# Experts in seven items instead of eight, three of them of 64, 32 and 32 places, with condition rows and experts' pieces fetched earlier

## The chip, the cores and the metric

The kernel runs on one core of a Trainium2 chip. The metric is the device time of one execution in microseconds (us), lower is better. All arithmetic is 32-bit float.

## The reference

Two groups of 128 tokens (context and latent) of width 1024 go through two layers with shared weights. Each layer computes a modulation from a condition vector, mixes tokens in three branches (differential attention, a long convolution, retention), projects, and ends in a mixture of 16 experts, which is what the change is about:

```python
def moe(h, w_router, b_router, w1, w3, w2):
    ...
    gate = ...          # top-1 group of four, top-2 experts inside it, per token
    a = jnp.einsum('bld,edf->blef', h, w1)          # D_MODEL 1024, D_FF 512
    b = jnp.einsum('bld,edf->blef', h, w3)
    act = jax.nn.silu(a) * b * gate[..., None].astype(h.dtype)
    return jnp.einsum('blef,efd->bld', act, w2)
```

With 256 tokens and two experts per token, an expert gets 32 tokens on average, and every expert's 6 MB of weights are needed in each layer.

## The kernel before

**Pieces and slots.** All weights come in pieces of 128 x 2048 floats (1 MB), fetched by SP (`fetch`, L578 to L585) in one fixed order, `PLAN` (L116): modulation pieces (`ada`), the projections (`proj`, units 0 to 29), six merges, four output units, four pieces of modulation part 5, then the 96 pieces of the experts (`moe`). `ring_table` (L138) gives each piece a slot and the count of `s_weights_used` that TensorE must have reached before the slot may be overwritten. There are 8 ring slots (`SLOTS`) and 6 lent ones (`LENT`), the latter made of tiles of the token-mixing stage. Dense pieces use the first 5 ring slots (`LEAST`), the opening's pieces all 8; the experts' pieces use all 14, the lent ones once the last merge is done (`END["merge", layer, 5]`). SP issues in order: a wait for one piece holds all behind it. Before the experts SP also waits for the stores of the stage before (`s_stored`, L596) and for the last chunk (`s_chunk_used`, L597).

**Chunks.** Ring slots 5 to 7 hold, during the token mixing, the condition rows, broadcast to 128 partitions (`cond_wide`, `raw`, L439 to L441), and the landings of 64 chunks of modulation weights, which DVE multiplies with the rows (`make_parts`, L1753). SP fetches chunks between dense pieces (`fetch_chunk`, L566); the first waits for `s_cond_ready` 2. In the opening POOL fetches the rows (L655) once all pieces of the opening are used (`MADE_FREE`, L654), ACT takes their tanh after unit 1 of the convolution (L1452), and DVE finishes them after unit 2 and its decay tables (L1886 to L1890).

**Opening of TensorE.** `first_units_of_first` (L822) computes units 0 to 3 as the modulation comes in, then `proj` (L794) runs units 4 to 29 with banks 0 to 3 in turn; DVE frees a bank when it has applied the convolution's taps to the unit.

**Experts.** Tokens are routed, experts 0 to 11 are sorted by their number of tokens (`sort`, L2217), and the work is cut into eight items (L42 to L50). An item is 128 places, which TensorE uses as stationary columns:

- a pair: two experts with 64 places each (items 0 and 1 the unsorted experts 12 to 15; items 4 to 6 sorted places 1 to 6)
- wide: the largest expert with 128 places (item 2)
- quad: the four smallest with 32 places each (item 3)
- single: one expert with 64 places (item 7), its weights split in two halves that run side by side in 64 columns each (`moe_in_extra` L1108, `moe_out_extra` L1151)

For each item `gather` (L1062) brings the tokens to their places; `moe_in` (L1087) multiplies them with the four pieces of w1 and w3 per expert in four quarters (two halves times banks 6 and 7), eight k-steps each, in each step one matmul per expert:

```python
for k in range(KT):
    for j in range(many):
        rows = slice(width * j, width * j + width)
        last = pe.matmul(bank[b][rows, half * 256:half * 256 + 256],
                         hgat[:, k, rows], w[j][:, k, :], ...)
```

ACT (tanh, L1630) and DVE (L2341, L2345) form the activation, `act_turn` (L1123) transposes it, `moe_out` (L1130) multiplies with the two pieces of w2 per expert in two halves of four f-steps, 512 columns each, and `combine` (L1175) adds the item to the output banks 0 to 3 through a matrix of places and gates. TensorE's order is in item p, gather p + 1, turn p, out p - 1 and combine (L1284 to L1298); in layer 0 it also does steps of the next layer's filter in items 3 to 6. The chain `seats`, `picks` (L2180, L2203) makes the place matrices on DVE, one pair of small operations per group and expert. An expert with more tokens than its room (`rooms`, L2241: 128 for the largest, 32 for the four smallest, else 64) gets extra blocks of 64 (`more_block`), which none does with these inputs.

`w[j]` of item p can be overwritten only after the whole quarter, since TensorE reports `many` pieces at once (L1106, L1143).

Of the kernel before, what the change touches and what calls it, by code (L numbers as in the profile page):

```python
# [17 lines left out]
ALU = mybir.AluOpType  # L18
# [3 lines left out]
P = 128  # L22
# [19 lines left out]
ITEM_KINDS = ("pair", "pair", "wide", "quad", "pair", "pair", "pair", "single")  # L42
# [3 lines left out]
ITEM_EXPERTS = ((12, 13), (14, 15), (0,), (8, 9, 10, 11), (1, 2), (3, 4), (5, 6), (7,))  # L46
# [3 lines left out]
ITEM_LAST = [2 if kind == "single" else len(e) for kind, e in zip(ITEM_KINDS, ITEM_EXPERTS)]  # L50
WIDE_ROOM, SMALL_ROOM = 128, 32

MORE = 2 * TOK // (BLOCK + 1)
# [26 lines left out]
LANDINGS = 3  # L80

# [56 lines left out]
def ring_table():  # L138

    pieces = [(item, c) for item in PLAN for c in range(PLAN_PIECES[item[0]])]  # L140
    done = [(item, c) for item in DONE for c in range(PLAN_PIECES[item[0]])]
    gone = {piece: n + 1 for n, piece in enumerate(done)}
    free, filled = [0] * (SLOTS + LENT), [0] * (SLOTS + LENT)
    slot, count, used = [], [], []
    for (kind, layer, _), c in pieces:
        lent = range(SLOTS, SLOTS + LENT) if kind == "moe" else ()
        own = SLOTS if kind == "moe" or (kind, layer, _) in OPENING else LEAST
        since = {at: free[at] for at in range(own)}
        since.update({at: max(free[at], END["merge", layer, 5]) for at in lent})
# [5 lines left out]
        free[at] = gone[(kind, layer, _), c]  # L155
    return slot, count, used
# [4 lines left out]
MADE_FREE = max(END[item] for n, item in enumerate(OPENING))  # L161
# [34 lines left out]
def y_end(layer, p, half):  # L196

    if p == PAIRS:
        return END["moe", layer, 0]
    return ff_end(layer, p + 1) + ITEM_OUT[p] // 2 * (half + 1)  # L200
# [92 lines left out]
def trunk_program(nc, row_scratch, cond_scratch, weights, mod_weights, cond_rows, experts, mod_params, params, consts, shared, x_in, k_cache, v_cache, s_cache,  # L293
                  y_out, k_out, v_out, s_out):
    with ExitStack() as ctx:
# [264 lines left out]
        def _(sp):  # L560
# [3 lines left out]
            chunk = 0  # L564

# [12 lines left out]
            def fetch(source):  # L578
                nonlocal n
                if USED[n]:  # L580

                    sp.wait_ge(s_weights_used, USED[n])
                slot = ring[:, SLOT[n], :] if SLOT[n] < SLOTS else lent[:, SLOT[n] - SLOTS, :]
                sp.dma_start(slot, source).then_inc(s_weights_in[SLOT[n]], 16)
                n += 1  # L585

            for kind, layer, number in PLAN:
                if kind != "moe":
# [7 lines left out]
                sp.wait_ge(s_stored, 16 * 4 * (layer + 1))  # L596
                sp.wait_ge(s_chunk_used, sum(CHUNKS[:layer + 1]))  # L597
# [8 lines left out]
                for p in range(ITEMS):  # L606
# [7 lines left out]
                    for part in (0, 2, 1, 3) if ITEM_KINDS[p] == "single" else range(4):  # L614
                        for j in range(many):
                            fetch(expert(p, j, part))
# [4 lines left out]
                for part in (4, 5):  # L621
                    fetch(expert(PAIRS, 0, part))
# [7 lines left out]
        def _(pool):  # L630
# [15 lines left out]
            for layer in range(DEPTH):  # L646
# [49 lines left out]
        def _(pe):  # L696
# [390 lines left out]
            def moe_in(layer, p):  # L1087
# [5 lines left out]
                width = P // many  # L1093
                for half in range(2):
                    for b in (6, 7):
# [12 lines left out]
            def moe_in_extra(layer):  # L1108

                pe.wait_ge(s_hgat_lo, ITEMS * layer + PAIRS + 1)  # L1110
                pe.wait_ge(s_hgat_hi, ITEMS * layer + PAIRS + 1)
                for b in (6, 7):
                    take(b)
                    w = piece(256), piece(256)
                    for k in range(KT):
                        for j in range(2):
                            last = pe.matmul(bank[b][64 * j:64 * j + 64, 0:256],  # L1117
                                             hgat[:, k, 64 * j:64 * j + 64], w[j][:, k, :],
                                             start=(k == 0), stop=(k == KT - 1),
                                             skip_group_check=True)  # L1120
                    last.then_inc(s_weights_used, 2)

            def act_turn(layer, p):  # L1123
                pe.wait_ge(s_act_ready, ITEMS * layer + p + 1)
                take(6)
                for f in range(4 if p < PAIRS else 2):
# [3 lines left out]
            def moe_out(layer, p):  # L1130
# [3 lines left out]
                width = P // many  # L1134
                for half in range(2):
                    w = [piece(512) for _ in range(many)]
                    take(5 - half)
                    for f in range(4):
                        for j in range(many):
                            rows = slice(width * j, width * j + width)  # L1140
# [3 lines left out]
                if p == 0:  # L1144
                    for b in range(4):
                        take(b)
                last = combine(s_y_lo, ITEMS * layer + p + 1, s_y_hi, PAIRS * layer + p + 1,
                               s_scat_ready, scat[p % 3], p == 0)
                last.then_inc(s_combined, 1)

            def moe_out_extra(layer):  # L1151

                n = ITEMS * layer + PAIRS + 1
                pe.wait_ge(s_actT_ready, n)
                w = piece(512), piece(512)
                take(5)
                for f in range(4):
                    for j in range(2):
                        last = pe.matmul(bank[5][64 * j:64 * j + 64, :],
                                         actT[PAIRS % 2][:, f % 2, 64 * (f // 2):64 * (f // 2) + 64],  # L1160
                                         w[j][:, f, :], start=(f == 0), stop=(f == 3),
                                         skip_group_check=True)
                last.then_inc(s_weights_used, 2)
                pe.wait_ge(s_scat_ready, n)
                pe.wait_ge(s_y_lo, n)
                for j in range(2):
                    r = slice(64 * j, 64 * j + 64)
                    for t in range(4):
                        last = pe.matmul(bank[2 * j + t // 2][:, (t % 2) * TOK:(t % 2 + 1) * TOK],
                                         ysb[r, t * P:(t + 1) * P], scat[PAIRS % 3][r, :],  # L1170
                                         start=False, stop=False, skip_group_check=True)
                        if t % 2:
                            last.then_inc(s_combined, 1)

            def combine(lo, count, hi, hi_count, scat_event, matrix, fresh):  # L1175
                pe.wait_ge(scat_event, count)
                for dt in range(KT):
                    if dt == 0:
                        pe.wait_ge(lo, count)
                    if dt == 4:  # L1180
# [4 lines left out]
                                     skip_group_check=True)  # L1185
                return last
# [42 lines left out]
            for layer in range(DEPTH):  # L1229
# [91 lines left out]
        def _(act_e):  # L1321
# [82 lines left out]
            for layer in range(DEPTH):  # L1404
# [40 lines left out]
                for u in range(U_HY, U_HY + 6):  # L1445
# [6 lines left out]
                    if layer == 0 and u == 1:  # L1452
# [173 lines left out]
                for p in range(ITEMS):  # L1626
                    n = ITEMS * layer + p
                    sc_e.wait_ge(s_weights_used, ff_end(layer, p) - ITEM_LAST[p])
                    wide = 512 if p < PAIRS else 256
                    sc_e.activation(th[:, 0:wide], bank[6][:, 0:wide], ACT.Tanh, scale=0.5).then_inc(  # L1630
                        s_ff_tanh, 1)
# [3 lines left out]
                    sc_e.activation(flat(actT[p % 2])[:, 0:wide], bank[6][:, 0:wide],  # L1635
                                    ACT.Copy).then_inc(s_actT_ready, 1)
# [33 lines left out]
        def _(dve):  # L1670
# [140 lines left out]
            for layer in range(DEPTH):  # L1811
# [60 lines left out]
                for u in range(U_HY, U_HY + 6):  # L1872
# [307 lines left out]
                def seats(p):  # L2180

                    many = 2 if ITEM_KINDS[p] == "single" else len(ITEM_EXPERTS[p])
                    ranks_, gates_ = (rank, gate) if p < FIXED_ITEMS else (sorted_rank, sorted_gate)
                    for g in range(GROUPS):
                        for j in range(many):
                            e = ITEM_EXPERTS[p][j % len(ITEM_EXPERTS[p])]
                            width = P // many
                            yield (g, slice(width * j, width * j + width), C("xf")[:, 0:width],
# [52 lines left out]
                def rooms():  # L2241
# [5 lines left out]
                    link(ts(extra, at, SORTED - 4.5, ALU.is_gt, float(SMALL_ROOM - BLOCK), ALU.mult))  # L2247
# [9 lines left out]
                def out_high(p):  # L2257
# [5 lines left out]
                    dve.wait_ge(s_y_hi, PAIRS * layer + p + 1)  # L2263
# [62 lines left out]
                for p in range(ITEMS):  # L2326
                    n = ITEMS * layer + p
                    wide_ff = 512 if p < PAIRS else 256
# [10 lines left out]
                    if n:  # L2339
                        dve.wait_ge(s_act_turned, n)  # L2340
                    link(stt(act[:, 0:wide_ff], th[:, 0:wide_ff], 1.0, bank[6][:, 0:wide_ff], ALU.add,  # L2341
                             ALU.mult))
                    dve.sem_inc(s_bank_free[6], 1)
                    dve.wait_ge(s_weights_used, ff_end(layer, p))
                    tt(act[:, 0:wide_ff], act[:, 0:wide_ff], bank[7][:, 0:wide_ff],  # L2345
                       ALU.mult).then_inc(s_act_ready, 1)
# [14 lines left out]
                    if p == PAIRS - 1:  # L2361
                        dve.wait_ge(s_more_known, layer + 1)
                        blocks = dve.value_load(ints[0:1, 0:1], min_val=0, max_val=MORE)

# [169 lines left out]
```

## Time and profile before

| | before |
| --- | --- |
| median of 3 runs | 1211.95 us (1210.23 to 1212.96) |
| the profiled execution, its own time | 1209.46 us |
| its span in the profile | 1207.7 us |
| mean granted TensorE clock, share of full speed | 0.978 |
| TensorE matmul busy (x records) | 1144.6 us (x6966) |
| VectorE busy | 510.8 us (42%) |
| ScalarE busy | 215.3 us (18%) |
| bytes moved by DMA | 351.51 MB, mean 291 GB/s |
| SP's fetches of experts' pieces | 108 to ring, 84 to lent slots, 1024 KB each |
| condition rows, issue to landing | 6.2 us |

PE is TensorE's matmul, PEld its weight load, DVE VectorE, ACT ScalarE, POOL GpSimd, SP SyncE; a `q` behind a name is the engine's sequencer. L1102 is line 1102. The profile shows each f32 matmul as two records, and their ends are modelled, so starts are the safer reading. PEclk is the TensorE clock that was granted (1.00 is 2.4 GHz). The chain lists what held the end, in order of time; a DMA in it counts from issue to landing.

### The profile page before, as it was taken

The numbers are of one execution on the slowest core, as the hardware profiler recorded it, in microseconds if no ns is written. First come the engines' busy times: TensorE is split into PE (matmuls) and PEld (weight loads), VectorE is DVE, ScalarE is ACT, GpSimd is POOL, SyncE is SP. The second block draws the span as 40 slices with busy tenths as digits, with TensorE's granted clock in tenths as the row PEclk, the third lists the DMA queues.
The fourth block names the chain that finished last, engine by engine and source line by source line (L and its number), as shares of the span: only waits on it lengthen the run. The fifth ranks groups of instructions, "written<-read, shape, count | busy, mean of one in ns | idle before, by whom it ended". The sixth has DMA issues, their size and how long they took to land.

```text
span 1207.7 us, 17513 instructions
## 1 busy us (share of the span) xinstructions
PE 1144.6 (95%) x6966; PEld 883.0 (73%) x6966; DVE 510.8 (42%) x1154; ACT 215.3 (18%) x452; POOL 41.2 (3%) x83
## 2 busy tenths in 40 slices
PE   6978999999999999989989999999999999998996
PEld 5667888878888775646548888888888877564653
DVE  2539877666736221111233876653252531111113
ACT  2240012232021100111124201223201210000011
POOL 1001110000000000000000111000000000000000
PEclk9998999999998999989999999999999899998999
DMA  9519874365459999999964578543434999999992
GB/s 384 219 70 347 310 283 172 142 261 223 183 205 423 421 421 386 422 420 421 420 261 161 180 279 276 188 161 132 139 140 177 418 421 420 371 422 420 421 420 101
DMA packets 55799, 351.51 MB, mean 291 GB/s; under 512 B 6960, under 2 KB 7136, under 8 KB 18336
## 3 DMA queue, kind: packets, MB, share of 16 engines
q1 hardware_dynamic: 51552, 337.75, 70.7%
q0 software_dynamic: 4160, 12.58, 2.8%
q8 instruction: 58, 0.95, 0.3%
q14 instruction: 29, 0.24, 0.1%
HBM read 346.08 MB, written 2.65 MB: 289 GB/s over the span
## 4 chain that ended last, share of the span: by engine, by line
PE 83%; DMA 11%; DVE 3%; ACT 2%; issue 1%; SPq 1%; DVEq 0%; ACTq 0%; POOLq 0%
PE bank L806 24%; PE bank L1102 12%; PE bank L1141 7%; PE bank L986 7%; PE bank L1007 5%; PE bank L801 5%; PE bank L1082 4%; PE bank L1182 4%; DMA lent<-in_experts 4%; DMA ring<-in_experts 4%; DMA ring<-in_weights 3%; PE bank L817 2%; PE bank L730 1%; PE bank L1117 1%; PE bank L1058 1%
## 5 line engine op out<-in xcount | busy, mean ns | idle before, releaser
L806 PE MATMUL bank<-h,ring 128*128 128x256 f32 x1472 | 327.4, 382 | 13.1 <-DMA ring<-in_weights 13.1
L806 PEld LDWEIGHTS bank<-h,ring 128*128 128x128 f32 x1472 | 279.0, 191 | 54.2 <-DMA ring<-in_weights 13.5
L1770 DVE SCALAR_TENSOR_TENSOR ring<-ring 128x1024 f32<-128x1024 f32 x128 | 151.7, 1223 | 17.5 <-DMA ring<-in_mod_weights 8.9
L1102 PE MATMUL bank<-lent,gates 128*64 128x256 f32 (+2 forms) x896 | 127.0, 380 | 2.3 <-ACT gates L1610 2.3
L1102 PE MATMUL bank<-ring,gates 128*64 128x256 f32 (+2 forms) x1024 | 121.0, 380 | 6.2 <-DMA ring<-in_experts 4.8
L1102 PEld LDWEIGHTS bank<-lent,gates 128*64 128x64 f32 (+2 forms) x896 | 82.6, 137 | 36.3 <-ACT gates L1610 2.8
L1102 PEld LDWEIGHTS bank<-ring,gates 128*64 128x64 f32 (+2 forms) x1024 | 80.0, 130 | 30.6 <-issue 6.8
L1141 PE MATMUL bank<-ring,gates 128*64 128x512 f32 (+2 forms) x304 | 83.7, 613 | 9.5 <-DMA lent<-in_experts 9.5
L1690 DVE SCALAR_TENSOR_TENSOR gates<-gates,bank 128x512 f32<-128x512 f32 (+1 forms) x16 | 10.5, 654 | 141.3 <-issue 108.9
L2262 DVE COPY uc<-bank 128x512 f32<-128x512 f32 x14 | 9.7, 692 | 132.4 <-PE bank L1141 132.4
L1141 PEld LDWEIGHTS bank<-ring,gates 128*64 128x64 f32 (+2 forms) x304 | 24.5, 135 | 54.2 <-issue 54.2
L1082 PE MATMUL bank<-uc,gates 128*128 128x128 f32 x512 | 60.4, 276 | 0.1
L1082 PEld LDWEIGHTS bank<-uc,gates 128*128 128x128 f32 x512 | 58.6, 192 | 0.7 <-DVE uc L1686 0.4
L986 PE MATMUL bank<-lent,ring 128*128 128x256 f32 x256 | 56.4, 380 | 0.0
L801 PE MATMUL bank<-ring,h 128*128 128x256 f32 x256 | 56.2, 379 | 0.0
L1007 PE MATMUL bank<-uc,ring 128*128 128x256 f32 x256 | 55.6, 379 | 0.0
L1141 PE MATMUL bank<-lent,gates 128*64 128x512 f32 (+2 forms) x176 | 55.0, 688 | 0.0
L1007 PEld LDWEIGHTS bank<-uc,ring 128*128 128x128 f32 x256 | 48.6, 190 | 6.6
L986 PEld LDWEIGHTS bank<-lent,ring 128*128 128x128 f32 x256 | 48.5, 190 | 6.5
L1182 PEld LDWEIGHTS bank<-gates,uc 128*128 128x128 f32 x224 | 41.6, 190 | 15.9 <-issue 10.8
L817 PE MATMUL bank<-h,ring 128*128 128x256 f32 x192 | 46.6, 403 | 6.6 <-ACT h L1346 6.6
L801 PEld LDWEIGHTS bank<-ring,h 128*128 128x128 f32 x256 | 48.2, 190 | 6.3
(268 smaller groups left out, 1141.8 us busy)
## 6 DMA issues: line engine op xcount, KB each, us to landing
ring<-in_experts SPq DMA_DIRECT2D x108, 1024.0 KB, 21.2
ring<-in_weights SPq DMA_DIRECT2D x96, 1024.0 KB, 6.5
lent<-in_experts SPq DMA_DIRECT2D x84, 1024.0 KB, 19.9
ring<-in_mod_weights SPq DMA_DIRECT2D x64, 512.0 KB, 5.6
lent<-lent POOLq DMA_DIRECT2D x48, 32.0 KB, 5.6
cst<-in_consts POOLq DMA_DIRECT2D x1, 1345.0 KB, 11.6
x<-in_x_in SPq DMA_DIRECT2D x1, 1024.0 KB, 5.0
ring<-in_cond_rows POOLq DMA_DIRECT2D x1, 1024.0 KB, 6.2
```

The lines of the kernel that those rows point to most:

```text
L730: last = pe.matmul(bank[b][32 * j:32 * j + 32, 0:256], condT[:, k, :], w[j][:, k, :], start=(k == 0), stop=(k == KT - 1), skip_group_check ...
L801: last = pe.matmul(bank[b][:, g * 256:(g + 1) * 256], h[:, k, g_cols(g)], w[:, k, :], start=(k == 0), stop=(k == KT - 1))
L806: last = pe.matmul(bank[b][:, c * TOK:(c + 1) * TOK], w[:, k, c * P:(c + 1) * P], h[:, k, :], start=(k == 0), stop=(k == KT - 1))
L817: last = pe.matmul(bank[u][:, c * TOK:(c + 1) * TOK], w[:, k, c * P:(c + 1) * P], h[:, k, :], start=(k == 0 and c == 0), stop=(k == KT - 1 ...
L986: last = pe.matmul(bank[b][:, c * TOK:(c + 1) * TOK], w[:, k, d * P:(d + 1) * P], src[:, k, :], start=(k == 0), stop=(k == 3))
L1007: last = pe.matmul(out[c], w[:, k, c * P:(c + 1) * P], merged[:, k, :], start=(k == 0), stop=(k == KT - 1))
L1058: last = pe.matmul(bank[b][:, c * P:(c + 1) * P], h[:, k, g_cols(n // 2)], ident, start=True, stop=True)
L1082: last = pe.matmul(bank[4 + half][:, c * P:(c + 1) * P], htok[:, g, k * P:(k + 1) * P], pick[p % 2][:, g, :], start=(g == 0), stop=(g == 1))
L1102: last = pe.matmul(bank[b][rows, half * 256:half * 256 + 256], hgat[:, k, rows], w[j][:, k, :], start=(k == 0), stop=(k == KT - 1), skip_g ...
L1141: last = pe.matmul(bank[5 - half][rows, :], actT[p % 2][:, f, rows], w[j][:, f, :], start=(f == 0), stop=(f == 3), skip_group_check=True)
L1182: last = pe.matmul(bank[dt // 2][:, (dt % 2) * TOK:(dt % 2 + 1) * TOK], ysb[:, dt * P:(dt + 1) * P], matrix, start=(fresh and dt % 2 == 0) ...
L1770: last = dve.scalar_tensor_tensor(out, w, 0.5, cond_wide[:, c, :], ALU.mult, ALU.mult, accum_out=mod_all[:, of, row, c:c + 1])
```

## The change

- Eight items become seven: pair, pair, triple, wide, triple, pair, triple. A triple is one expert with 64 places and two with 32, in columns 0 to 63, 64 to 95 and 96 to 127. Quad and single are gone, with `moe_in_extra` and `moe_out_extra`. The number of pieces stays 96 per layer; an item's share is 4 per expert in and 2 out.
- The six smallest sorted experts have room 32 instead of the four smallest.
- The last item's combine reports each bank by itself.
- The opening's pieces use ring slots 0 to 4 and lent slots 0 to 2, so that slots 5 to 7 are free for the condition rows. POOL fetches these after `END["ada", 0, 1]`; the cache loads into the lent tiles wait for the opening's end. ACT's tanh comes after unit 0, DVE's step after unit 1, ahead of unit 2 and the decay tables.
- Modulation part 5 may use slots 5 to 13 like the experts, once the last merge is done. The wait for the stores moves ahead of it, the wait for the chunks ahead of the first piece that goes to slots 5 to 7.

```diff
-ITEM_KINDS = ("pair", "pair", "wide", "quad", "pair", "pair", "pair", "single")
+ITEM_KINDS = ("pair", "pair", "triple", "wide", "triple", "pair", "triple")
+WIDTHS = {"pair": (64, 64), "triple": (64, 32, 32), "wide": (128,)}
...
-ITEM_EXPERTS = ((12, 13), (14, 15), (0,), (8, 9, 10, 11), (1, 2), (3, 4), (5, 6), (7,))
+ITEM_EXPERTS = ((12, 13), (14, 15), (1, 6, 7), (0,), (2, 8, 9), (4, 5), (3, 10, 11))
...
+OPENING_LENT = (SLOTS, SLOTS + 1, SLOTS + 2)
...
-    for (kind, layer, _), c in pieces:
-        lent = range(SLOTS, SLOTS + LENT) if kind == "moe" else ()
-        own = SLOTS if kind == "moe" or (kind, layer, _) in OPENING else LEAST
-        since = {at: free[at] for at in range(own)}
-        since.update({at: max(free[at], END["merge", layer, 5]) for at in lent})
+    for (kind, layer, number), c in pieces:
+        since = {at: free[at] for at in range(LEAST)}
+        if (kind, layer, number) in OPENING:
+            since.update({at: free[at] for at in OPENING_LENT})
+        elif kind == "moe" or (kind, number) == ("ada", 5):
+            since.update({at: max(free[at], END["merge", layer, 5]) for at in range(LEAST, SLOTS + LENT)})
...
-MADE_FREE = max(END[item] for n, item in enumerate(OPENING))
+OPENING_END = max(END[item] for item in OPENING)
...
+        if SLOT[n] in range(LEAST, SLOTS) and not given[layer]:
+            sp.wait_ge(s_chunk_used, sum(CHUNKS[:layer + 1]))
+            given[layer] = True
...
+        if (kind, number) == ("ada", 5):
+            sp.wait_ge(s_stored, 16 * 4 * (layer + 1))
...
-        sp.wait_ge(s_stored, 16 * 4 * (layer + 1))
-        sp.wait_ge(s_chunk_used, sum(CHUNKS[:layer + 1]))
...
-        pool.wait_ge(s_weights_used, MADE_FREE)
         pool.dma_start(raw, cond_rows.broadcast_to([P, 2 * D])).then_inc(s_cond_moved, 16)
-        pool.wait_ge(s_mod_ready, ada_at(0, 1) + 1)
+        pool.wait_ge(s_weights_used, OPENING_END)
...
-        for j in range(many):
-            rows = slice(width * j, width * j + width)
+        for j, rows in enumerate(ITEM_ROWS[p]):
...
+        if by_bank and dt % 2 and dt < KT - 1:
+            last.then_inc(s_combined, 1)
...
-        for p in range(PAIRS):
+        for p in range(ITEMS):
             moe_in(layer, p)
-            gather(layer, p + 1)
+            if p < PAIRS:
+                gather(layer, p + 1)
...
-        moe_in_extra(layer)
-        act_turn(layer, PAIRS)
-        moe_out(layer, PAIRS - 1)
-        moe_out_extra(layer)
+        moe_out(layer, PAIRS)
...
-        if layer == 0 and u == 1:
+        if layer == 0 and u == 0:
...
-            if layer == 0:
-                dve.wait_ge(s_cond_tanh, 2)
-                stt(flat(cond_wide), flat(cond_wide), 1.0, raw, ALU.add, ALU.mult).then_inc(
-                    s_cond_ready, 1)
-                dve.wait_ge(s_cond_ready, 2)
+        if layer == 0 and u == 1:
+            dve.wait_ge(s_cond_tanh, 2)
+            stt(flat(cond_wide), flat(cond_wide), 1.0, raw, ALU.add, ALU.mult).then_inc(
+                s_cond_ready, 1)
+            dve.wait_ge(s_cond_ready, 2)
...
-        many = 2 if ITEM_KINDS[p] == "single" else len(ITEM_EXPERTS[p])
         ranks_, gates_ = (rank, gate) if p < FIXED_ITEMS else (sorted_rank, sorted_gate)
         for g in range(GROUPS):
-            for j in range(many):
-                e = ITEM_EXPERTS[p][j % len(ITEM_EXPERTS[p])]
-                width = P // many
-                yield (g, slice(width * j, width * j + width), C("xf")[:, 0:width],
+            for e, rows in zip(ITEM_EXPERTS[p], ITEM_ROWS[p]):
+                yield (g, rows, C("xf")[:, 0:rows.stop - rows.start],
...
-        link(ts(extra, at, SORTED - 4.5, ALU.is_gt, float(SMALL_ROOM - BLOCK), ALU.mult))
+        link(ts(extra, at, SORTED - SMALL - 0.5, ALU.is_gt, float(SMALL_ROOM - BLOCK), ALU.mult))
```

## Rows read from the trace of the kernel before

**Rows 1.** The page, busy time, share of the span and records of TensorE's matmuls

```profile
PE 1144.6 (95%) x6966; PEld 883.0 (73%) x6966; DVE 510.8 (42%) x1154; ACT 215.3 (18%) x452; POOL 41.2 (3%) x83
```

**Rows 2.** The chain that ended last, opening: start us, us, what

```profile
40.87 3.66 PE bank L730 x64
...
66.20 6.18 DMA ring<-in_cond_rows
...
90.40 5.54 DMA ring<-in_weights
```

**Rows 3.** Timeline, opening: start us, us, engine line op tiles, shapes [idle before, releaser]

```profile
74.21 1.00 ACT L1449 ACTIVATE uc<-bank,par 128x256 f32<-128x256 f32 x2
...
87.71 2.29 DVE L1690 SCALAR_TENSOR_TENSOR ring<-ring 128x2048 f32<-128x2048 f32 x1
...
95.99 16.42 PE L806 MATMUL bank<-h,ring 128*128 128x256 f32 x64 [13.09 <-DMA ring<-in_weights]
```

**Rows 4.** Windows: stretch, length, busy PE PEld DVE ACT POOL, PEclk, DMA share, GB/s

```profile
83.00:96.00 13.00, 0.01 (x1) 0.01 (x1) 8.88 (x13) 5.21 (x16) 0.51 (x1) 0.66 0.38 143
430.00:440.00 10.00, 10.00 (x49) 7.64 (x44) 3.61 (x17) 0.00 (x0) 0.00 (x0) 1.00 1.01 420
```

**Rows 5.** The chain that ended last, from the merges to the experts of both layers

```profile
329.12 6.99 PE bank L986 x32
...
386.50 14.03 PE bank L1102 x128
...
406.30 14.03 PE bank L1102 x128
...
424.71 7.02 PE bank L1141 x32
431.73 3.65 PE bank L1182 x16
435.38 13.81 PE bank L1102 x64
...
464.09 3.63 PE bank L1102 x64
...
617.04 2.94 PE bank L1169 x16
...
964.10 14.03 PE bank L1102 x128
...
1193.96 4.16 PE bank L790 x16
```

**Rows 6.** SP's timeline at the first expert's piece; landings of L584, 300 to 640

```profile
357.32 1.53 SPq L584 DMA_DIRECT2D ring<-in_experts  x3
...
DMA to landing us min/median/max: 4.7/18.3/29.3
```

**Rows 7.** Timeline of TensorE at four changes of line (PE matmul, PEld weight load)

```profile
448.60 0.59 PE L1102 MATMUL bank<-ring,gates 128*128 128x256 f32 x2
448.82 0.36 PEld L1072 LDWEIGHTS bank<-cst,uc 128*128 128x128 f32 x2
...
463.50 0.59 PE L1182 MATMUL bank<-gates,uc 128*128 128x256 f32 x2
464.02 0.42 PE L1102 MATMUL bank<-ring,gates 128*32 128x256 f32 x3
...
464.02 0.12 PEld L1102 LDWEIGHTS bank<-ring,gates 128*32 128x32 f32 x3 [0.33 <-issue]
...
431.13 0.60 PE L1141 MATMUL bank<-lent,gates 128*64 128x512 f32 x2
431.66 0.48 PE L1182 MATMUL bank<-gates,uc 128*128 128x256 f32 x1
...
327.63 1.24 PE L986 MATMUL bank<-lent,ring 128*128 128x256 f32 x5
328.71 0.27 PE L1017 MATMUL bank<-cst,sm 128*16 128x128 f32 x1
```

More of the change, by code:

```diff
@@ L49 @@
 ITEM_OUT = [2 * len(e) for e in ITEM_EXPERTS]
-ITEM_LAST = [2 if kind == "single" else len(e) for kind, e in zip(ITEM_KINDS, ITEM_EXPERTS)]
-WIDE_ROOM, SMALL_ROOM = 128, 32
-MORE = 2 * TOK // (BLOCK + 1)
+ITEM_ROWS = [[slice(sum(WIDTHS[kind][:j]), sum(WIDTHS[kind][:j + 1])) for j in range(len(WIDTHS[kind]))]
+             for kind in ITEM_KINDS]
+WIDE_ROOM, SMALL_ROOM, SMALL = 128, 32, 6
+MORE = 8
 OVER = (TOK - 1 - SMALL_ROOM) // BLOCK + 1
@@ L154, in ring_table @@
         used.append(since[at])
-        free[at] = gone[(kind, layer, _), c]
+        free[at] = gone[(kind, layer, number), c]
     return slot, count, used
@@ L198, in y_end @@
     if p == PAIRS:
-        return END["moe", layer, 0]
+        return END["moe", layer, 0] - ITEM_OUT[p] // 2 * (1 - half)
     return ff_end(layer, p + 1) + ITEM_OUT[p] // 2 * (half + 1)
@@ L564, in _ @@
             chunk = 0
+            given = [False] * DEPTH
             def fetch_chunk():
@@ L613, in _ @@
                                                         max_val=SORTED - 1)
-                    for part in (0, 2, 1, 3) if ITEM_KINDS[p] == "single" else range(4):
+                    for part in range(4):
                         for j in range(many):
@@ L621, in _ @@
                 for part in (4, 5):
-                    fetch(expert(PAIRS, 0, part))
+                    for j in range(len(ITEM_EXPERTS[PAIRS])):
+                        fetch(expert(PAIRS, j, part))
             for c in range(4):
@@ L1106, in moe_in @@
                         last.then_inc(s_weights_used, many)
[L1108 to L1121, printed above, removed]
             def act_turn(layer, p):
@@ L1125, in act_turn @@
                 take(6)
-                for f in range(4 if p < PAIRS else 2):
+                for f in range(4):
                     last = pe.transpose(bank[6][:, f * P:(f + 1) * P], act[:, f * P:(f + 1) * P], ident)
@@ L1133, in moe_out @@
                 many = len(ITEM_EXPERTS[p])
-                width = P // many
                 for half in range(2):
@@ L1138, in moe_out @@
                     for f in range(4):
-                        for j in range(many):
-                            rows = slice(width * j, width * j + width)
+                        for j, rows in enumerate(ITEM_ROWS[p]):
                             last = pe.matmul(bank[5 - half][rows, :], actT[p % 2][:, f, rows], w[j][:, f, :],
@@ L1146, in moe_out, with combine @@
                         take(b)
-                last = combine(s_y_lo, ITEMS * layer + p + 1, s_y_hi, PAIRS * layer + p + 1,
-                               s_scat_ready, scat[p % 3], p == 0)
+                last = combine(s_y_lo, ITEMS * layer + p + 1, s_y_hi, ITEMS * layer + p + 1,
+                               s_scat_ready, scat[p % 3], p == 0, p == PAIRS)
                 last.then_inc(s_combined, 1)
[L1151 to L1175, printed above, removed]
+            def combine(lo, count, hi, hi_count, scat_event, matrix, fresh, by_bank=False):
                 pe.wait_ge(scat_event, count)
@@ L1627, in _ @@
                     n = ITEMS * layer + p
[L1628 to L1631, printed above, removed]
+                    sc_e.wait_ge(s_weights_used, ff_end(layer, p) - len(ITEM_EXPERTS[p]))
+                    sc_e.activation(th, bank[6][:, :], ACT.Tanh, scale=0.5).then_inc(s_ff_tanh, 1)
                     if p + 1 < ITEMS:
@@ L1634, in _ @@
                     sc_e.wait_ge(s_act_turned, n + 1)
-                    sc_e.activation(flat(actT[p % 2])[:, 0:wide], bank[6][:, 0:wide],
-                                    ACT.Copy).then_inc(s_actT_ready, 1)
+                    sc_e.activation(flat(actT[p % 2]), bank[6][:, :], ACT.Copy).then_inc(s_actT_ready, 1)
                     sc_e.wait_ge(s_actT_ready, n + 1)
@@ L2262, in out_high @@
                     dve.tensor_copy(ysb[:, 512:1024], bank[4][:, :]).then_inc(s_y_hi, 1)
-                    dve.wait_ge(s_y_hi, PAIRS * layer + p + 1)
+                    dve.wait_ge(s_y_hi, ITEMS * layer + p + 1)
                     dve.sem_inc(s_bank_free[4], 1)
@@ L2327, in _ @@
                     n = ITEMS * layer + p
-                    wide_ff = 512 if p < PAIRS else 256
                     if p + 1 < ITEMS:
@@ L2340, in _ @@
                         dve.wait_ge(s_act_turned, n)
-                    link(stt(act[:, 0:wide_ff], th[:, 0:wide_ff], 1.0, bank[6][:, 0:wide_ff], ALU.add,
-                             ALU.mult))
+                    link(stt(act, th, 1.0, bank[6][:, :], ALU.add, ALU.mult))
                     dve.sem_inc(s_bank_free[6], 1)
                     dve.wait_ge(s_weights_used, ff_end(layer, p))
-                    tt(act[:, 0:wide_ff], act[:, 0:wide_ff], bank[7][:, 0:wide_ff],
-                       ALU.mult).then_inc(s_act_ready, 1)
+                    tt(act, act, bank[7][:, :], ALU.mult).then_inc(s_act_ready, 1)
                     dve.wait_ge(s_act_ready, n + 1)
@@ L2363, in _ @@
                         blocks = dve.value_load(ints[0:1, 0:1], min_val=0, max_val=MORE)
+                out_high(PAIRS)
                 def more_block(layer, i):
```

2 lines of the change are left out of this document (removed).

## Prediction

> **What bounds the kernel now.** I read the page's shares first, then the chain that ended last, the timeline of the opening, the windows, and last single matmuls. TensorE is busy 95% of the span [rows 1]: its stream is the path, except where something holds it, and the chain shows where. In the opening the chain leaves TensorE for the condition rows' DMA (66.20 for 6.18), comes through decay tables to one DVE step of 2.29 that ends at 90.00, and goes back by a weight piece issued at 90.40 and landed in 5.54 [rows 2, 3]. TensorE idles 13.09 us of it, and since its clock falls to 0.66 [rows 4] its next 64 matmul records take 16.42 us [rows 3] instead of the 13.81 that 64 of this shape take elsewhere [rows 5]. In the experts' stage (386.50 to 619.98, 233.5 us; in the second layer 964.10 to 1193.96, 229.9 us) the chain is TensorE again [rows 5], while transfers run at 420 GB/s with a DMA share of 1 [rows 4], so that a piece of 1.049 MB takes 2.50 us. This stage has two limits close together: its matmuls, and its 96 pieces.
>
> The profile counts each f32 matmul as two records. A pair (two experts of 64 places side by side) has 128 records in 14.03 us, the wide item 64 in 13.81, a quarter of the quad 64 in 3.63 [rows 5]. So two or four narrow matmuls of one width run at once, and an item costs one full array's time, whatever it holds. The change builds on that.
>
> **Part 1, the opening.** SP stands before its first chunk until the condition step is done; the next dense piece is queued behind it [rows 2]. Now the rows' DMA waits only for the second modulation part, done at 44.5 [rows 2], 21.7 us before 66.20. It lands at 44.5 + 6.2 = 50.7, or, with two dense pieces in flight, at 55.7. ACT's tanh now follows unit 0 and may delay unit 1 by about 1 us; DVE's 2.29 follow unit 1, still before unit 2's matmuls end (about 65.6). So the piece that held TensorE can go out near 64 and land 5.5 us later, before TensorE asks for it at 95.99 - 13.09 = 82.90. Late next is the rest of DVE's chain: from 74.21 [rows 3] to 90.00 less the 2.29 moved out, now begun at 65.6, so unit 3's bank is free after its 2.03 us of taps near 81.2, and TensorE wants it at 89.8. Gain 13.1 + (16.4 - 13.8) = 15.7. Bounds: 10.9, if TensorE runs into DVE, whose own shift is only 90.00 - 79.1, and 15.7, which I take. POOL's cache loads stay behind the opening as they were. The opening's pieces sit in three lent slots in place of ring slots, the same number: nothing.
>
> **Part 2, earlier pieces.** SP issues in order; today it passes the last modulation pieces one by one behind the output projection, and the first expert's piece leaves at 357.32 [rows 6]. Now ten pieces may go when the last merge is done, 336.11 [rows 5]; the waits for stores and chunks that move ahead with them are satisfied earlier. But there are 14 slots, all full by then: later pieces wait for item 0's first quarter, done at 390.0. Today's queue reaches the fifteenth expert piece at 357.3 + 14 x 2.5 + 1.8 (the parameters' 0.75 MB) = 394. So 4 us of the 21 are left, for transfers alone. On a path bound by TensorE they are worth 0; if transfers set the end they are already in rival 1. POOL's two broadcasts of 512 KB share the queue, and TensorE needs their work 30 us later: 0.
>
> **Part 3, seven items, if a triple cost as much as a pair.** Without waits for DMA: item 0 takes 19.8 (386.50 to 406.30), a later one with a pair in and a pair out 29.1 (406.30 to 435.38), with the wide item in 28.7 (435.38 to 464.09) [rows 5], out of the wide 28.9; the last in-step has no gather behind it, 14.0 + 1.2 (the turn, no longer hidden) + 7.0 + 3.65 = 25.9; the last out 7.0 + 0.8 (copy) + 3.65 = 11.5. In all 19.8 + 29.1 + 29.0 + 28.7 + 28.9 + 29.0 + 25.9 + 11.5 = 201.9, and with 4.4 for filter steps in layer 0 206.3. Against 229.9 and 233.5: -28.0 and -27.2. Combining bank by bank adds only increments; a triple's 12 picks instead of 8 lie on DVE, busy 3.61 of 10 us [rows 4]; layer 1's first dense pieces now wait for half of the last out, still 12 us before they are used: 0 each. The routing of the reference's inputs puts at most 28 (layer 0) and 23 tokens (layer 1) on the six smallest sorted experts, so rooms of 32 call no extra block.
>
> **Part 4, what a triple costs.** It alternates 64, 32 and 32 columns, which no row shows. But each change of shape can be read. Full to full: records start 0.21 apart, and the weights of the next load at 448.82, 0.01 after the last record's start at 448.81. Full to 32 columns: 463.71 to 464.02, 0.31, and its LDWEIGHTS starts no earlier than its matmul. 64 columns to full, 512 moved: 431.14 to 431.66, 0.52 where 0.43 is usual [rows 7]. The surcharge is the same 0.09 whether 32 or 128 columns are to be loaded, so it isn't the load; it looks like a stop until the old shape has left the array. One row speaks against it: a transpose of 16 columns follows full matmuls after 0.22, with no gap [rows 7].
>
> If 64 to 32 is such a change, the 64 never overlaps the 32s. A k-step is 0.216 + 0.31 + 0.216 + 0.31 = 1.05 us instead of 0.44; 32 of them take 33.6, not 14.03: +19.6. An out-step is 2 x 0.43 + 2 x 0.52 = 1.90; 8 of them 15.2, not 7.02: +8.2. Together 27.8 per triple, 83.4 per layer. From below the cost is 0 (full overlap). From above each change waits for a matmul's whole 0.38 us, 5.7 more per triple: 33.5. I take 27.8: of all rows, those of a change are nearest. The Trainium skill, "TensorEngine Tiling (Array Packing)", Tiling Modes, says that changing the tiling mode, not just the tile, drains the engine, and lists 128x64 and 128x32 as two modes: by this rule the sum stands as it is. The same section calls tiles independent, loading and multiplying in parallel; by that alone a triple costs a pair, and the sum is rival 1's.
>
> **Sum**, against this execution's 1209.46 (span 1207.7): layer 0 -27.2 + 83.4 = +56.2, layer 1 -28.0 + 83.4 = +55.4, opening -15.7: +95.9, 1305.4. The median shown lies 2.5 above that execution: 1308.
>
> **Rival 1, the widths overlap (faster).** For: pairs and quads do, and the three tiles share no column. Against: no weights are loaded ahead across a change of shape. Then transfers decide. At 390.0 there are 82 pieces to issue; the last lands at 390.0 + 4.7 (the shortest landing [rows 6]) + 81 x 2.50 = 597.2, and half an out 3.5, copy 0.8 and combine 3.65 follow: 605.2 for 619.98, -14.8. Layer 1: 967.6 + 4.7 + 202.5 + 8.0 = 1182.8 for 1193.96, -11.2. With the opening 1167.8, as a median 1170 (1150 if slots and transfers never bind; 1192 with added waits and a lower clock). Its opposite begins where a triple costs (27.2 + 28.0 + 15.7) / 6 = 11.8 us more than a pair: beyond that point the change is slower.
>
> **Rival 2, overlap with a surcharge.** 2 x 0.09 in each of 32 + 8 steps, 7 us per triple: the stage takes 206.3 + 21 = 227, so some 5 us less than now, or the same with its waits. The opening alone is sure: 1209.5 - 15.7, median 1196 (1175 to 1212).
>
> **Rival 3, one width after the other, no stop.** A k-step 0.87 and an out-step 1.74: +20.7 per triple, 34.9 + 34.1 - 15.7: median 1265. It is the low end of my own case.
>
> **Chances.** The forecast, with rival 3 inside it, 0.57; its own range is 1255 to 1342. Rival 1 0.32. Rival 2 0.09, 0.01 of it within 0.2%, which is what a measurement of this kernel can tell from nothing. Anything else 0.02, half of it same, half slower. So faster 0.40, same 0.02, slower 0.58. The range has to hold rival 1: 1160 to 1335, with under 0.1 outside it.
>
> **What would show it.** Right: in a triple, starts 0.22 and 0.31 apart in turn, a quarter of 8.4 us with 48 records, LDWEIGHTS of the first 32 beside its own matmul, the DMA share under 0.9 in triples, no TensorE wait near 83. Rival 1: quarters of 3.5 us, 420 GB/s to the stage's end, and TensorE waiting for pieces in the last item. The forecast is wrong if a triple's quarter takes under 6 us; part 1 if TensorE still waits for a dense piece before 110.

## The result and the profile after

The changed kernel takes 1321.03 us (median; 1319.96 to 1322.32), the kernel before 1211.09 us (1208.37 to 1212.96): a ratio of 1.091, 95% interval 1.088 to 1.094. It is slower. The forecast was 1308 (range 1160 to 1335), and slower with a chance of 0.58. The profiled execution took 1322.08 with a span of 1320.3, against 1305.4 in the prediction's sum.

The page's line of busy time, to be held against [rows 1]:

```profile
PE 1285.1 (97%) x6862; PEld 869.6 (66%) x6862; DVE 505.6 (38%) x1140; ACT 210.5 (16%) x442; POOL 41.0 (3%) x83
```

TensorE has 104 records fewer than before and is busy 140.5 us longer, so a record takes longer on average.

The chain that ended last, from the experts of layer 0 and the triples' place in layer 1 (start us, us, what), which answers to [rows 5]:

```profile
368.94 14.03 PE bank L1108 x128
...
407.15 7.02 PE bank L1130 x32
...
417.82 36.21 PE bank L1108 x192
...
469.08 13.81 PE bank L1108 x64
...
487.12 15.88 PE bank L1130 x48
...
1061.76 36.21 PE bank L1108 x192
...
1307.23 3.54 PE bank L798 x16
```

A pair still takes 14.03 into the hidden layer and 7.02 out of it, the wide item 13.81. A triple takes 36.21 and 15.88, together 52.09. From its first experts' matmul to what follows its last combination, layer 0's stage runs from 368.94 to 667.65 and layer 1's from 1012.88 to 1307.23: 298.7 and 294.4 us, 65.2 and 64.5 more than before.

Inside a triple, the timeline of TensorE's weight loads and, further on, of its matmuls out of the hidden layer (start us, us, engine line op tiles, shapes, count, idle before):

```profile
420.01 0.19 PEld L1108 LDWEIGHTS bank<-ring,gates 128*64 128x64 f32 x2 [0.41 <-issue]
420.59 0.14 PEld L1108 LDWEIGHTS bank<-ring,gates 128*32 128x32 f32 x4 [0.39 <-issue]
421.15 0.19 PEld L1108 LDWEIGHTS bank<-ring,gates 128*64 128x64 f32 x2 [0.41 <-issue]
...
487.05 1.62 PE L1130 MATMUL bank<-ring,gates 128*64 128x512 f32 x3
488.06 0.62 PE L1130 MATMUL bank<-lent,gates 128*32 128x512 f32 x1
...
489.04 1.62 PE L1130 MATMUL bank<-ring,gates 128*64 128x512 f32 x3
```

One k-step goes from 420.01 to 421.15 (1.131 by the records' exact starts), one f-step from 487.05 to 489.04. The two 32s load together (four weight loads in 0.14 us), but the 64 stands by itself: the widths take turns, and the loads of the new width start only when the turn comes.

Windows of after (stretch, length, busy PE PEld DVE ACT POOL, PEclk, DMA share, GB/s), as [rows 4]:

```profile
83.00:96.00 13.00, 13.00 (x62) 11.45 (x61) 12.13 (x22) 1.31 (x3) 0.00 (x0) 1.00 0.42 139
343.00:350.00 7.00, 6.78 (x42) 6.12 (x40) 2.69 (x8) 2.75 (x10) 0.00 (x0) 1.00 1.01 418
420.00:440.00 20.00, 20.00 (x108) 6.03 (x108) 0.00 (x0) 0.00 (x0) 0.00 (x0) 1.00 0.77 298
```

The hole of the opening is filled, at full clock. Experts' pieces already fill the DMA engines at 343. In this part of a triple the share is 0.77; over all six stretches of triples' matmuls into the hidden layer it is 0.71 to 0.86, as SP waits for TensorE to free slots. No wait of TensorE for an expert's piece is left in the list of its waits.

### The profile page after: what moved, and what is told of

It reads as the page before. It is cut to its first block, busy times and chain, and to the rows that moved or that the text cites. A ratio compares the mean times of both kernels' runs of the same rounds, so it can differ in the third digit from the quotient of the medians.

```text
span 1320.3 us, 17253 instructions
## 1 busy us (share of the span) xinstructions
PE 1285.1 (97%) x6862; PEld 869.6 (66%) x6862; DVE 505.6 (38%) x1140; ACT 210.5 (16%) x442; POOL 41.0 (3%) x83
## 4 chain that ended last, share of the span: by engine, by line
PE 94%; DMA 2%; DVE 2%; ACT 1%; issue 0%; SPq 0%; DVEq 0%; ACTq 0%
PE bank L1108 25%; PE bank L814 23%; PE bank L1130 11%; PE bank L994 6%; PE bank L1015 4%; PE bank L809 4%; PE bank L1090 4%; PE bank L1147 4%; PE bank L825 3%; DMA ring<-in_weights 2%; PE bank L738 1%; PE bank L1066 1%; PE bank L798 1%; PE bank L939 1%; PE bank L877 1%; DVE rinv L1912 1%
## 5 line engine op out<-in xcount | busy, mean ns | idle before, releaser
L814 PE MATMUL bank<-h,ring 128*128 128x256 f32 x1472 | 324.8, 380 | 0.0
L1108 PE MATMUL bank<-ring,gates 128*64 128x256 f32 (+2 forms) x1344 | 244.5, 389 | 2.3 <-ACT gates L1575 2.3
L1108 PE MATMUL bank<-lent,gates 128*64 128x256 f32 (+1 forms) x704 | 120.3, 388 | 1.4 <-ACT gates L1575 1.4
L1652 DVE SCALAR_TENSOR_TENSOR gates<-gates,bank 128x512 f32<-128x512 f32 x14 | 9.6, 688 | 235.7 <-issue 177.6
L1130 PE MATMUL bank<-lent,gates 128*64 128x512 f32 (+2 forms) x320 | 98.2, 600 | 0.0
L1108 PEld LDWEIGHTS bank<-lent,gates 128*64 128x64 f32 (+1 forms) x704 | 46.3, 125 | 62.8 <-issue 51.0
L1130 PE MATMUL bank<-ring,gates 128*64 128x512 f32 (+1 forms) x192 | 71.1, 607 | 0.0
L1130 PEld LDWEIGHTS bank<-lent,gates 128*64 128x64 f32 (+2 forms) x320 | 24.4, 133 | 53.5 <-issue 53.5
L1594 ACT ACTIVATE gates<-bank 128x512 f32<-128x512 f32 x14 | 8.4, 597 | 293.0 <-PE bank L1108 293.0
L1147 PEld LDWEIGHTS bank<-gates,uc 128*128 128x128 f32 x224 | 41.6, 190 | 15.9 <-issue 10.9
L1147 PE MATMUL bank<-gates,uc 128*128 128x256 f32 x224 | 51.9, 385 | 0.0
```

Of the source, the lines that this page charges most:

```text
L814: last = pe.matmul(bank[b][:, c * TOK:(c + 1) * TOK], w[:, k, c * P:(c + 1) * P], h[:, k, :], start=(k == 0), stop=(k == KT - 1))
L1130: last = pe.matmul(bank[5 - half][rows, :], actT[p % 2][:, f, rows], w[j][:, f, :], start=(f == 0), stop=(f == 3), skip_group_check=True)
L1147: last = pe.matmul(bank[dt // 2][:, (dt % 2) * TOK:(dt % 2 + 1) * TOK], ysb[:, dt * P:(dt + 1) * P], matrix, start=(fresh and dt % 2 == 0) ...
```

## The experiments

The theory after the result (called A in what follows) was that of the forecast: a triple is dear because its three tiles have two widths, and each change of width stops the array; the opening gains 15.7; the earlier pieces are worth nothing, as TensorE sets the pace. The rival (B) held that the transfers still set the stage's end somewhere, so that part 2 is worth something. Each part was first run alone.

**The opening alone.** The kernel before with part 1 (slots and POOL's order as in the change). Of the edits shown, the second is where ACT takes the tanh of the condition rows, the third where DVE finishes them:

```diff
+OPENING_LENT = (SLOTS, SLOTS + 1, SLOTS + 2)
...
-                    if layer == 0 and u == 1:
+                    if layer == 0 and u == 0:
...
+                    if layer == 0 and u == 1:
+                        dve.wait_ge(s_cond_tanh, 2)
+                        stt(flat(cond_wide), flat(cond_wide), 1.0, raw, ALU.add, ALU.mult).then_inc(
+                            s_cond_ready, 1)
+                        dve.wait_ge(s_cond_ready, 2)
```

> The kernel before with part 1 alone (condition rows after the second modulation part, opening in lent slots, tanh after unit 0, DVE step after unit 1). My step: TensorE's 13.1 us wait and the slow clock behind it go, -15.9 us as in the changed kernel's trace (the unit after the dense pieces starts at 96.9 instead of 112.8), so 1195 us. Rival, the gain is given back later because DVE and its chunks fall behind: between 1197 and 1211 us.

1193.94 us against 1208.28 for before in these runs, ratio 0.986 (0.982 to 0.991): -14.3, near the 15.9 expected and outside the rival's 1197 to 1211. The chain of the opening no longer leaves TensorE (start us, us, what):

```profile
68.92 27.63 PE bank L808 x128
96.55 0.44 PE bank L864 x4
96.99 13.82 PE bank L803 x64
```

The 64 matmul records that took 16.42 [rows 3] are the second half of the 128 in 27.63, so 13.8. In the kernel before, the clock was 0.66 in the idle stretch ahead of them and 0.50 from 96 to 100, over their first records; from 104 on it was 1.00.

**The earlier pieces alone.** The kernel before with part 2, the wait for the chunks moved ahead of the first piece that goes to slots 5 to 7, and the wait for the stores ahead of modulation part 5. `n > 20` leaves out the opening's pieces, which use those slots too in this kernel:

```diff
+                if SLOT[n] in range(LEAST, SLOTS) and n > 20 and not given[layer]:
+                    sp.wait_ge(s_chunk_used, sum(CHUNKS[:layer + 1]))
+                    given[layer] = True
...
+                if (kind, number) == ("ada", 5):
+                    sp.wait_ge(s_stored, 16 * 4 * (layer + 1))
...
-                sp.wait_ge(s_stored, 16 * 4 * (layer + 1))
-                sp.wait_ge(s_chunk_used, sum(CHUNKS[:layer + 1]))
```

> The kernel before with part 2 alone (modulation part 5 and the experts may use all slots once the last merge is done). Theory A, TensorE sets the pace of the stage: no change, 1211 us. Theory B, the transfers' start counts: the last piece of the quad's in-step lands at 476.36 in the trace of before and would land up to 9 us earlier, so the waits of 1.9 and 4.9 us per layer and the low clock behind the second (0.66) go: 6 to 8 us per layer, 1196 to 1200 us.

1208.63 us, ratio 0.999 (0.997 to 1.002): nothing, which is A's number. Windows of this run, same columns as above:

```profile
336.00:357.00 21.00, 21.00 (x99) 18.50 (x98) 5.16 (x17) 5.21 (x16) 0.00 (x0) 1.00 1.01 417
430.00:440.00 10.00, 10.00 (x48) 8.79 (x48) 3.46 (x17) 0.00 (x0) 0.00 (x0) 1.00 1.01 421
440.00:460.00 20.00, 20.00 (x111) 13.96 (x110) 3.35 (x8) 2.77 (x5) 0.00 (x0) 1.00 0.75 290
```

Between 336 and 357 the queue moves at 417 GB/s where the kernel before moved 195. It gives the lead back twice: at 370 to 386 its share is 0.78, when the slots are full and the first item frees none, and at 440 to 460, in the wide item, 0.75 where the kernel before has 0.97. TensorE's waits for experts' pieces are nearly what they were: 8.0 us in the matmuls out of the hidden layer and 5.1 in those into it, before 9.5 and 4.8. The chain shows what they hang on, first in the kernel before, then with part 2:

```profile
468.40 7.96 DMA ring<-in_experts
...
499.51 22.26 DMA lent<-in_experts
```

```profile
466.48 7.28 DMA lent<-in_experts
...
496.92 22.48 DMA lent<-in_experts
```

The first of each two is the last piece that the quad's matmuls into the hidden layer wait for, the second the one that those out of it wait for. Each is issued only when a quarter has ended and freed its slots (the quad's first quarter at 467.73 before and 465.81 here, the next pair's first at 498.84 and 496.24), so an earlier start of the queue doesn't bring it sooner. So the result is theory A's number, but not its reason: TensorE still waits for pieces, at moments that the slots set. That is read from the chain; no run with more slots was made.

**One width after the other.** The changed kernel, in each quarter of a triple (a k-loop of 8 steps) and each half out of it (an f-loop of 4 steps) the 64's whole loop first, and then that of the two 32s:

```diff
+                groups = [places_[:1], places_[1:]] if len(places_) == 3 else [places_]
+                return [(k, j, rows) for group in groups for k in range(steps) for j, rows in group]
```

> The changed kernel, but in a triple all k-steps (f-steps) of the 64-place expert come first and then those of the two 32-place experts: same matmuls, 2 changes of shape in a quarter instead of 16. Theory (one width after the other, plus a stop at each change): a quarter 8 x 0.432 + 8 x 0.438 + about 0.26 = 7.2 us instead of 9.05, an out-half 7.2 instead of 7.9, so 8.8 us less per triple, 53 in all: 1268 us. Rival, each change of shape costs nothing and a triple is slow for having three streams of weights: unchanged, 1321 us. Rival, only the change costs and unlike widths do overlap: there is no overlap to see in this order either, so it tells nothing of that.

1264.62 us, ratio 1.046 (1.041 to 1.050). The chain, a triple's matmuls in and out:

```profile
419.24 28.70 PE bank L1113 x192
...
481.03 14.27 PE bank L1134 x48
```

Same records, same data; the width now changes 8 times in and 4 out, twice for each quarter and half, where it changed 64 and 16 times. 42.97 us per triple instead of 52.09: 9.1 us for 68 changes, 0.13 each, and 54.7 in all six triples. The rival, that the change costs nothing and three streams of weights are slow (1321), falls. The other 21.9 above a pair's 21.05 are the second width's own turn, since a 64 and a 32 never share the array, with the 12 changes that are left (some 1.6 by the same price); rival 3's price for the turn was 20.7. Within the group the 32s do run at once; the timeline shows both starting together, 0.21 apart from the next two:

```profile
437.36 0.38 PE L1113 MATMUL bank<-ring,gates 128*32 128x256 f32 x1
...
437.37 0.38 PE L1113 MATMUL bank<-lent,gates 128*32 128x256 f32 x1
...
437.58 0.38 PE L1113 MATMUL bank<-ring,gates 128*32 128x256 f32 x1
```

**One width only.** The changed kernel, the 64 places computed as two tiles of 32 columns of the same expert, so that a triple is four equal tiles:

```diff
+                if ITEM_KINDS[p] == "triple":
+                    return [(j, slice(at, at + 32)) for j, at in ((0, 0), (0, 32), (1, 64), (2, 96))]
+                return list(enumerate(ITEM_ROWS[p]))
```

> The changed kernel, but in a triple the 64-place expert is given to two tiles of 32 columns, both with its weights, beside the two 32-place experts: four matmuls of one shape in a step, no change of shape. Theory: a quarter costs what the quad's did, 3.63 us, the triple costs a pair, and the transfers set the end of the stage as in rival 1: 1167 to 1175 us. Rival, three unlike experts in an item are slow whatever their shape: over 1300 us.

1173.76 us, ratio 0.970 (0.966 to 0.975). This version beats both kernels: before by 34.5 (1208.28 in these runs) and the change by 147 us. Its chain, a triple in and out, and the end of layer 0's stage:

```profile
417.48 13.95 PE bank L1114 x256
...
464.52 7.05 PE bank L1136 x64
...
528.41 22.25 DMA ring<-in_experts
...
556.70 26.21 DMA ring<-in_experts
...
590.45 0.86 PE bank L789 x2
```

With 80 records more than the grouped triple, the triple takes 21.00 us, what a pair takes. Now the transfers are in the chain, and TensorE waits for experts' pieces 28.2 us in all, 14.3 before. The DMA share over 368 to 590 is 0.99 at 411 GB/s.

**The same without part 2,** and then **without parts 1 and 2** (SP's waits, the slots and, in the second, the condition step as in the kernel before).

> Seven items with the triples as four 32-wide tiles (the kernel of the run with four 32s, 1173.8 us), but the experts' first pieces issued where the kernel before issues them. Theory A, the experts' stage is bound by its transfers and slots, and earlier pieces only fill slots that would be filled anyway: within 2 us of it, 1172 to 1176. Theory B, where the stage is bound by its transfers, each byte fetched before the stage counts, so that part 2 has a worth here that it had not with eight items: 1178 to 1186, with longer DMA waits in TensorE's rows of the experts' stage.

> The seven items with four 32-wide tiles, with neither the new opening nor the earlier pieces. By the sum of parts: the run with late pieces plus 15.7 of the opening, so 1188 to 1192 by theory A, 1194 to 1202 by theory B. A rival: the opening's microseconds are partly lost where the transfers bind, as the queue has less time before the stage; then the difference between this run and the one with late pieces is under 12 us.

1183.75 us (1182.33 to 1186.54) and 1199.83 us (1195.71 to 1202.66; ratio to before 0.990, 0.987 to 0.994). So with seven items part 2 is worth some 9 to 10 us: 10.0 by the medians, which are of two chips (the kernel before took 1208.28 and 1209.14 on them), and 9.1 by the traces, where layer 0's stage is 5.9 us longer without it and layer 1's 3.2. Theory A, whose number was at most 1176, falls for this kernel. The opening is worth 16.1 here, so nothing of it is seen to be lost. A window of each, first with and then without part 2 (columns as above):

```profile
336.00:357.00 21.00, 20.79 (x123) 19.20 (x122) 9.07 (x38) 6.43 (x19) 0.53 (x1) 0.92 1.01 420
440.00:460.00 20.00, 20.00 (x94) 15.92 (x91) 3.66 (x14) 0.63 (x2) 0.00 (x0) 1.00 1.01 422
```

```profile
336.00:357.00 21.00, 20.78 (x121) 19.26 (x120) 8.73 (x36) 6.88 (x20) 0.53 (x1) 0.92 0.82 333
```

With part 2 the queue also runs at 384 GB/s from 320 to 330, where without it it has 251. Summed over 320 to 370 it moves 19.6 MB against 15.6: 3.9 MB, 9.3 us at 420 GB/s. Without part 2 the layer-0 stage ends at 596.83 instead of 590.45. Some of the lead is given back between 368 and 410 (399 GB/s with part 2, 420 without), but none in the wide item, where eight items lost it: the share there stays 1.01. A full queue alone doesn't tell what a lead is worth: the kernel before moved 416 GB/s over 368 to 590, at a share of 1.01, and part 2 gave it nothing. Why the slots hold out here was not tried by itself; what differs is the triple, with more pieces, ahead of the wide item, and that there is no quad.

**The price of a change by itself.** The kernel before, its wide item's odd k- and f-steps done as two tiles of 64 columns of the same expert. The filled columns stay the same, so no overlap is lost or won; only the tile's width changes, 32 times in and 8 out:

```diff
+                if ITEM_KINDS[p] == "wide" and step % 2:
+                    return [(0, slice(0, 64)), (0, slice(64, 128))]
```

> The kernel before, but in its widest item every other k-step (and f-step) is done as two tiles of 64 columns of the same expert, so that the tile's width changes at each step while the columns that are filled stay the same, and no overlap of tiles is lost. Theory, the price of a change is a gap of 0.31 (256 columns) plus a longer first record: about 0.14 us for each of 32 changes, so the item's matmuls into the hidden layer take 18 to 19 us instead of 13.8 and those out of it 7.5 to 8.5 instead of 6.9; the whole time within 1208 to 1222, as the item waits for its transfers. Rival, the price of a change is seen only between 64 and 32 (other halves of the array): 13.8 and 6.9 as before.

One execution, 1215.82 us, 7 above the median of before (1209.14, up to 1212.86) and in the expected range; the finding rests on the trace. The chain of the wide item, in and out:

```profile
434.22 19.19 PE bank L1108 x96
...
488.93 8.06 PE bank L1146 x24
```

5.38 us more than 13.81 for 32 changes, 0.17 each, and 1.19 more than 6.87 for 8, 0.15 each; the expectation for the first (18 to 19) was just short. The rival, no price between these widths, falls. The weight loads show both widths in turn:

```profile
440.01 0.30 PEld L1108 LDWEIGHTS bank<-lent,gates 128*128 128x128 f32 x2 [0.39 <-issue]
440.64 0.20 PEld L1108 LDWEIGHTS bank<-lent,gates 128*64 128x64 f32 x4 [0.33 <-issue]
441.22 0.30 PEld L1108 LDWEIGHTS bank<-lent,gates 128*128 128x128 f32 x2 [0.39 <-issue]
```

The records' exact starts divide the price in two. After the last record of the old width the next starts 0.31 later instead of 0.21, at every change tried (128 and 64 here, 64 and 32 in the triples, both ways). Then the first record of the new width lasts 0.32 (128 columns), 0.27 (64) or 0.24 (32) until the second.

## Why the prediction was right, and what it missed

**The sign and the mechanism** were right. The trace shows three of the marks that the forecast named: the first 32's weight load beside its own matmul, a DMA share under 0.9 in triples (0.71 to 0.86), no wait near 83. Two came out larger: starts are 0.31 apart at a change, as named, but 0.27 and 0.24 between changes where 0.22 was named, and a quarter of a triple takes 36.21 / 4 = 9.1 us, where 8.4 was named. The stated range says little by itself, since it was made to hold the faster rival too; 1321.03 also lies in the forecast's own range, 1255 to 1342.

**The mis-sized term** is part 4's k-step, "0.216 + 0.31 + 0.216 + 0.31 = 1.05 us". The 0.31 was read rightly, but the 0.216 after it is the spacing of records whose weights were loaded ahead. After a change nothing was. The first record starts with its own load; the load of the second starts 0.055 us (64 columns) or 0.028 (32) after that of the first, and the second record 0.21 after its load. So the two start 0.266 and 0.240 apart, and a k-step takes 1.131; in the same way an f-step takes 1.985, not 1.90. The rows for it stood in the prediction ("its LDWEIGHTS starts no earlier than its matmul"), but only the gap was priced. Per triple 36.21 + 15.88 - 21.05 = 31.0 instead of 27.8; six times that is 186.2 instead of 166.8. These 19.4 us are more than the whole miss of 1322.08 - 1305.4 = 16.7; the rest of both stages came out 1.3 shorter than summed, and what lies ahead of the first stage 17.6 shorter instead of 15.7.

**Part 1**: the steps came about as worked out. The rows' DMA is issued at 44.6 and lands 9.4 us later (54.0; 50.7 or 55.7 were named), DVE's step ends at 63.10, the piece goes out at 63.50 (64), and unit 3's taps end at 80.99 (81.2). The hole and the slow records are gone. The line that follows them starts at 112.84 before (95.99 + 16.42 and 0.44 of four other records) and at 96.91 now: 15.9 earlier, predicted 15.7. The experts' stage begins 17.6 earlier than before. The other 1.7 come just ahead of it and were not forecast: from the last merge matmuls to the first expert's, the kernel before takes 22.8 us at a clock of 0.85, the change 21.1 at 0.92, and so does the run with the opening alone. Why the clock differs there was not tried. The gain shows alone (-14.3), and with four 32s (-16.1).

**Part 2**: nothing is seen of it in this change; no TensorE wait for an expert's piece is left. The bound that the prediction gave, 4 us of lead per layer where transfers set the end, compares with 5.9 and 3.2 in the two layers of the seven items with four 32s. The reason that it gave for nothing, a path bound by TensorE, holds for the triples of two widths; with eight items it isn't the whole of it, as the run with part 2 alone shows. That it was "already in rival 1" was right.

**Part 3**: take the three triples' 93.1 from the stages, and 205.6 and 201.3 are left; predicted 206.3 and 201.9. Picks and the half-way release cost nothing, as costed.

**Rival 1** had a chance of 0.32 and is false for tiles of two widths, but its sum is that of the kernel with four 32s: 1170 forecast, 1173.76 measured. Its layer-0 stage was to end at 605.2 - 15.7 = 589.5 and ends at 590.45, in part by luck: it takes 221.9 us where 218.7 were worked out, but begins 17.9 earlier instead of 15.7. The second takes 223.8 where 218.7 were worked out. Rival 2's own premise, overlap with a surcharge, is seen nowhere. Rival 3's time without a stop (1265) is that of the grouped order (1264.6), where few changes are left, though not none.

**The Trainium skill**'s rule in "TensorEngine Tiling (Array Packing)", Tiling Modes, that a change of mode drains the engine, agrees with all changes between tiles of 128, 64 and 32 columns in these runs: 128x64 and 128x32, for one, change places at 0.31 us instead of 0.21, and their tiles never run together though they share no column. The row that spoke against it, a transpose of 16 columns behind full matmuls at 0.22 [rows 7], stands unexplained; no run tried that width. Its sentence on independent tiles holds within one width: two 64s, or four 32s, at the price of one (21.05 and 21.00 us).

The gains of the seven items, then, are real, and were lost in one place. Of 1209 us, the items alone with equal tiles give 9, the opening 16 and the earlier pieces 10; that the triples have two widths takes back 147.

## What to carry to other kernels

Pack an array with tiles of one width, and if the parts differ, split the larger to the smaller's width: 64 + 32 + 32 columns cost 52.1 us, 32 + 32 + 32 + 32 cost 21.0, for the same data. If two widths are needed, run each one's loop to its end rather than alternate: 43.0 instead of 52.1. An earlier start of the transfers was worth nothing with eight items, where it was given back at full slots, and 9 to 10 us with seven, so a part that was measured at nothing is to be measured again after the rest of the stage has changed.

## What the runs showed of the hardware that was not expected

- A change of width costs twice: 0.09 us of stop, the same for 128, 64 and 32 columns, and a longer first record, by about 0.10, 0.05 and 0.02 us for 128, 64 and 32 columns (0.320, 0.266 and 0.240 instead of 0.214 to 0.216). The second part follows the new tile's columns; the first does not.
- Two tiles of different widths on different columns take turns. A triple in which each width runs by itself takes 42.97 us, twice a pair's 21.05.
- Four times as many matmul records of a quarter of the columns each cost next to nothing: a triple's 256 records take 13.95 us, the wide item's 64 records 13.81.
